# Attention rounds on TensorE: the older unit's value products ahead of the turning of probabilities

## The chip, the cores and the metric

The kernel runs on one core of a Trainium2 chip. The metric is the device time of one execution in microseconds (us), the slowest core's, which here is the only one. The profile comes from one further execution on the same kind of chip, recorded by the hardware profiler.

## What is computed

One forward pass at batch 1, 256 tokens and width 1024, in float32, through two blocks. The first has one layer: a mixer of forgetting attention (8 heads) and stick-breaking attention (8 heads), a cross-attention to 256 memory rows (4 heads of 256), and a mixture of 16 experts. The second has two layers, each a mixer of four groups and a gated feed-forward; a second stream of 256 context tokens runs beside the first in layer 0 only. Only the attentions matter here. Cut to what matters:

```python
def _forgetting_attention(q, k, v, f_logit):          # "fox", 8 heads of 64, blocks of 128 queries
    logits = einsum('bhqd,bhkd->bhqk', q_blk, kh) * scale + c_blk[..., None] - c[:, :, None, :]
    p = softmax(where(kpos <= qpos, logits, -inf)); return einsum('bhqk,bhkd->bhqd', p, vh)

def _memory_cross_attention(...):                     # "cross", 4 heads of 256, 256 memory rows
    p = softmax(einsum('bshd,bmhd->bhsm', q, k) * 256 ** -0.5)
    o = einsum('bhsm,bmhd->bshd', p, v)

# second block, each layer: groups A, C and D, 4 heads each
window_gqa(...)            # A: scores within a band and over the context, softmax with a sink, values
diff_weights(...)          # C: two softmaxes of 32-wide heads, w = p[0] - lam * p[1], values
neighbourhood_attn(...)    # D: 8x16 neighbourhood with a bias, and the context, softmax, values
```

## The kernel before

Each engine has a program of its own, written out in order, and they meet only at semaphores. An engine carries out its instructions in that order, so whatever stands behind a waiting instruction waits too. The names below ending in `_ready`, `_done` or `_turned` are such signals.

The four softmax attentions ("fox", "cross", "mix" of layer 0 and "mix" of layer 1) share one routine per engine: `pe_attention` on TensorE (PE), `act_attention` on ScalarE (ACT), `dve_attention` on VectorE (DVE). The work is cut into **units**: a block of 128 queries of one head or of two. fox has 8 units, cross 8, mix layer 0 has 32 (stream 0: C 8, A 4, D 4, with 512 keys; stream 1 the same with 256 keys), mix layer 1 has 16 (C 8, A 4, D 4, 512 keys). A unit has one or two score matrices (`subs`) and one or two probability matrices (`parts`): fox, A and D have two of each; C has two score matrices and one part; cross one of each. A **group** is the units whose outputs share PSUM bank 0 (in cross, banks 0 and 1 in turn).

The routines run in **steps**, step i being one pass of the loop over all units and three more. In step i

- PE writes the scores of unit i (L1051, extra terms L1055); does a small turn for the modulation vectors (L749, "ada"); turns the probabilities of unit i-2 with the identity matrix, 128x128 block by block, into bank 2 or 3 (L1067); multiplies the turned probabilities of unit i-3 with the values into the group's bank (L1084); then does what `fill` brings (ada products L742 in the first steps, and matmuls of the two norms, L1329, L1365, L1380);
- DVE takes the row maximum of unit i (L1126, for A with the sink L1129, L1130), then scales the probabilities of unit i-1 (L1144, or L1148 and L1150 for C), then, when a group of cross, A or D is complete, makes the low half of its output (L1157);
- ACT does the exponentials of unit i (L1097), copies the turned probabilities of unit i-2 from PSUM into `work` or `prob_turned` (L1109), and empties the bank of a complete group (L1171, L1175, L1179).

Who waits for whom, as far as the change touches it:

- a turning waits for its scaled probabilities (`probs_ready`, DVE) and for the ACT copy of the part two before it (`pT_ready`), because parts alternate between banks 2 and 3;
- value products wait for the copy of the last part of their unit (`pT_ready`), and in a new group for the bank being emptied: by ACT (`act_out`), after cross, A or D by DVE too (`dve_out`);
- the exponentials of unit i write into one of four buffers `prob(s)`. The score matrix four before must have been turned (`probs_turned`). With two score matrices a unit that is the turning of unit i-2, which PE does in the same step;
- scores wait for the exponentials four score matrices back (`exp_ready`; three back in cross).

In C, value products come only in every second step, for two units at once. After each attention the next stage waits for its last group; after the mixes these are the output projections ("wout2", L663 to L665).

Of the kernel before, what the change touches and what calls it, by code (L numbers as in the profile page):

```python
# [14 lines left out]
P = 128  # L15
# [204 lines left out]
def mixer_program(nc, a, out, counts):  # L220
# [6 lines left out]
    with ExitStack() as ctx:  # L227
# [3 lines left out]
        def signal(name):  # L231
            return Signal(ctx, nc, name, counts)
# [42 lines left out]
        bank = [ctx.enter_context(nc.psum_tensor(f"bank{i}", [P, 512], F32)) for i in range(4)]  # L275
# [3 lines left out]
        def const(name):  # L279
            off, n = CONST_AT[name]  # L280
            v = cst[:, off:off + n]
            return v.broadcast_to([P, P]) if n == 1 else v

        ident = const("ident")
# [64 lines left out]
        probs_ready = signal("probs_ready")  # L349
        probs_turned = signal("probs_turned")  # L350
        pT_ready = signal("pT_ready")
# [71 lines left out]
        def scores(qk, nk, extra=()):  # L423
            return dict(qk=qk, nk=nk, extra=extra)

        def part(sub, o, vals, lam=None):
            return dict(sub=sub, pv=[(o, vals)], lam=lam)
# [12 lines left out]
        def out_at(g, h, t):  # L440
            return bank[g["bank"]][head_rows(h), ((h % 4) // 2) * S + t * P:((h % 4) // 2) * S + t * P + P]

        fox_units, cross_units, mix_units = [], [], [[], []]
        for h in range(0, FOX_H, 2):
            if h % 4 == 0:
                g = group(("fox", h // 4))
            for t in range(ST):
                nk = (t + 1) * P
                subs, parts = [], []
# [7 lines left out]
        for h in range(X_HEADS):  # L457
            g = group(("cross", h), 2)
            for t in range(ST):
                s = scores([(xq[:, 2 * h + c, t * P:(t + 1) * P], xk[:, 2 * h + c, :]) for c in range(2)], S)  # L460
                pv = [(bank[g["bank"]][:, c * S + t * P:c * S + t * P + P],
                       [xv[:, b, (2 * h + c) * P:(2 * h + c + 1) * P] for b in range(ST)]) for c in range(2)]
                parts = [dict(sub=0, pv=pv, lam=None)]
                cross_units.append(dict(subs=[s], parts=parts, now=parts, group=("cross", h), last=t == 1))
        for l in range(LAYERS):
            for stream in range(2 if l == 0 else 1):
                lo = stream * S
                nk = 2 * S - lo
# [3 lines left out]
                for h in range(0, 4, 2):  # L472
                    for t in range(ST):
                        waiting = []
                        for x in (h, h + 1):
                            subs = []
# [3 lines left out]
                            parts = [part(0, out_at(g, x, t), [vc2[:, b, x * HD:(x + 1) * HD] for b in blocks], l)]  # L480
# [4 lines left out]
                for pair in ((0, 3), (1, 2)):  # L485
                    for t in range(ST):
                        subs, parts = [], []
                        for i, h in enumerate(pair):
                            kv = slice((h // 2) * HD, (h // 2) * HD + HD)
                            extra = []  # L490
                            if stream == 0:
# [5 lines left out]
                                                 last=pair == (1, 2) and t == 1,  # L497
                                                 sink=slice(l * 4 + pair[0], l * 4 + pair[1] + 1, step)))
                g = group(("D", l, stream))
                for h in range(0, 4, 2):  # L500
                    for t in range(ST):
                        subs, parts = [], []
                        for x in (h, h + 1):
                            extra = []
                            if stream == 0:
# [4 lines left out]
                                                 last=h == 2 and t == 1))  # L510
# [16 lines left out]
        prob = lambda s: work[:, (s % NP_) * 512:(s % NP_) * 512 + 512]  # L527
# [227 lines left out]
        def pe_ada_turn_left(pe):  # L755
            while ada_turn_left:
                pe_ada_turn(pe, ada_turn_left.pop())
# [282 lines left out]
        def pe_attention(pe, units, phase, fill):  # L1040

            ring, first = score_ring(phase), units[0]["s"][0]
            for i in range(len(units) + 3):
                if i < len(units):
                    unit = units[i]
                    for n in range(len(unit["subs"][0]["qk"])):
                        for s, sc in zip(unit["s"], unit["subs"]):
                            if n == 0 and s - first >= ring:
                                pe.wait_ge(*exp_ready.at(s - ring))
                            q, k = sc["qk"][n]  # L1050
                            last = pe.matmul(score_bank(phase, s)[:, 0:sc["nk"]], q, k, start=n == 0,  # L1051
                                             stop=n == len(sc["qk"]) - 1)
                    for s, sc in zip(unit["s"], unit["subs"]):
                        for left, right, c0, width in sc["extra"]:
                            last = pe.matmul(score_bank(phase, s)[:, c0:c0 + width], left, right, start=False, stop=True,  # L1055
                                             skip_group_check=True)
                    last.then_inc(*scores_ready.mark(unit["u"]))
                pe_ada_turn_left(pe)
                if 2 <= i < len(units) + 2:
                    unit = units[i - 2]  # L1060
                    nb = unit["subs"][0]["nk"] // P
                    for p in unit["parts"]:
                        pe.wait_ge(*probs_ready.at(p["p"]))
                        if p["p"] >= 2:
                            pe.wait_ge(*pT_ready.at(p["p"] - 2))
                        for b in range(nb):
                            last = pe.transpose(bank[2 + p["p"] % 2][:, b * P:(b + 1) * P],  # L1067
                                                prob(p["s"])[:, b * P:(b + 1) * P], ident)
                        last.then_inc(*probs_turned.mark(p["p"]))
                if i >= 3 and units[i - 3]["now"]:  # L1070
                    unit = units[i - 3]
                    g = groups[unit["group"]]
                    pe.wait_ge(*pT_ready.at(unit["now"][-1]["p"]))
                    if g["no"] >= g["banks"]:
                        emptied = by_no[g["no"] - g["banks"]]
                        pe.wait_ge(*act_out.at(("group", emptied)))
                        if emptied[0] in ("cross", "A", "D"):
                            pe.wait_ge(*dve_out.at(("group", emptied)))
                    for n in range(len(unit["now"][0]["pv"])):
                        nb = len(unit["now"][0]["pv"][n][1])  # L1080
                        for b in range(nb):
                            for p in unit["now"]:
                                o, vals = p["pv"][n]
                                last = pe.matmul(o, vals[b], by_block(p["p"])[:, b, :], start=b == 0, stop=b == nb - 1)  # L1084
                    last.then_inc(*pv_done.mark(unit["u"]))
                fill(i)

        def act_attention(act, units, phase, fill=lambda i: None):
# [955 lines left out]
        def _(pe):  # L2044
# [16 lines left out]
            pe.wait_ge(*dve_misc.at("forget"))  # L2061
            pe.wait_ge(*dve_misc.at("cond"))
            pe_attention(pe, fox_units, "fox", lambda i: pe_ada_step(pe, "fox", i))
            pe.wait_ge(*act_out.at(("group", ("fox", 1))))
            pe.wait_ge(*exp_ready.at(fox_units[-1]["s"][-1]))
# [13 lines left out]
            for j in range(4):  # L2079
                pe_tile(pe, ("xq", j), lambda c: pe_late(("xattn",))(pe, c) if j == 0 else None)  # L2080
                if j == 0:
                    pe_norm(pe, ("xattn",))
            pe.wait_ge(*dve_out.at(("xq", 3)))
            pe_attention(pe, cross_units, "cross", lambda i: pe_ada_step(pe, "cross", i))
            pe.wait_ge(*dve_out.at(("group", ("cross", 3))))
            for j in range(4):
# [25 lines left out]
            for l in range(LAYERS):  # L2112
# [21 lines left out]
                def fill(i, l=l):  # L2134
# [3 lines left out]
                    run_plan(l, "pe")(pe, i)  # L2138

                pe_attention(pe, mix_units[l], ("mix", l), fill)  # L2140
                for step in range(len(mix_units[l]) + 3, 60):
                    run_plan(l, "pe")(pe, step)
# [385 lines left out]
```

## Time and profile before

| | |
|---|---|
| median of 3 runs | 1779.58 us (1769.25 to 1780.74) |
| the profiled execution | 1777.42 us, of which its span is 1775.4 us |
| PE matmul busy | 1649.5 us, 93% of the span |
| DVE, ACT busy | 920.4 us, 688.5 us |
| share of the chain that ended last on PE | 84% |
| the four softmax attentions, us from the span's start | fox 105 to 147, cross 284 to 315, mix layer 0 800 to 915, mix layer 1 1464 to 1537 |

Times of rows are microseconds from the span's start. A row of the timeline is one merged set of instructions, with its start, its duration and, in brackets, how long the engine stood idle before it and what released it.

### The profile page before, as it was taken

To read this page: it belongs to the slowest core of one execution; us is meant where nothing else is said; L and a number is where in the kernel's file an instruction comes from. 1 tells how busy PE (TensorE), PEld (TensorE's weight loads), DVE (VectorE), ACT (ScalarE), POOL (GpSimd) and SP (SyncE) were. 2 spreads that over 40 slices of the span, in tenths; PEclk is the share of its full clock that TensorE was granted. 3 is DMA by queue.
4 is the path that set the end of the run, shared out by engine and by line. 5 is a ranking of instruction groups with operands and counts; after the bars stand their busy time and mean duration, and the time that the engine had idled before them with its cause. 6 is when DMAs were issued, how large, how long until landed. Compare 5 with 4: busy or idle time off the path is not lost.

```text
span 1775.4 us, 26046 instructions
## 1 busy us (share of the span) xinstructions
PE 1649.5 (93%) x11189; PEld 1427.8 (80%) x11189; DVE 920.4 (52%) x1249; ACT 688.5 (39%) x985; POOL 224.8 (13%) x203
## 2 busy tenths in 40 slices
PE   6999999999999998999688999999997998889997
PEld 5986898999999986875456878878876894789997
DVE  4621654665655553876745433323226767465554
ACT  4524543444433333225642322222223426543433
POOL 3001100020000013990200000000000690000000
PEclk8998999999999998999788999999998998989999
DMA  7466457355455533244204243343333330145552
GB/s 271 144 214 213 136 173 258 122 146 188 165 166 178 179 119 119 95 150 160 24 24 143 95 142 119 119 139 104 117 118 92 119 102 18 44 131 183 190 167 72
DMA packets 228892, 242.28 MB, mean 136 GB/s; under 512 B 13033, under 2 KB 222409, under 8 KB 228777
## 3 DMA queue, kind: packets, MB, share of 16 engines
q1 hardware_dynamic: 226672, 238.02, 40.8%
q0 software_dynamic: 1568, 2.37, 1.4%
q8 instruction: 89, 1.46, 0.3%
q10 hardware_dynamic: 536, 0.22, 0.1%
q14 instruction: 27, 0.21, 0.0%
HBM read 239.54 MB, written 1.05 MB: 136 GB/s over the span
## 4 chain that ended last, share of the span: by engine, by line
PE 84%; DVE 8%; ACT 4%; issue 2%; DMA 1%; ACTq 0%; POOL 0%; DVEq 0%
PE bank L663 21%; PE bank L665 20%; PE bank L664 20%; PE score_banks L1051 2%; PE bank L1084 2%; PE score_banks L1597 2%; DVE small L1126 2%; PE score_banks L1598 2%; PE score_banks L1599 2%; PE bank L1067 1%; PE bank L719 1%; PE score_banks L1055 1%; PE bank L720 1%; PE bank L721 1%; PE bank L742 1%
## 5 line engine op out<-in xcount | busy, mean ns | idle before, releaser
L652 DVE TENSOR_TENSOR w_lo<-raw,w_hi 128x2048 fp32r<-128x2048 f32 (+1 forms) x175 | 405.4, 2321 | 299.9 <-ACT w_hi L638 299.4
L663 PE MATMUL bank<-xn_hi,w_hi 128*128 128x256 f32 (+1 forms) x1248 | 416.5, 334 | 16.0 <-DVE w_lo L652 8.0
L664 PE MATMUL bank<-xn_lo,w_hi 128*128 128x256 f32 (+1 forms) x1248 | 412.4, 330 | 0.0
L665 PE MATMUL bank<-xn_hi,w_lo 128*128 128x256 f32 (+1 forms) x1248 | 412.2, 330 | 0.0
L638 ACT ACTIVATE w_hi<-raw 128x2048 fp32r<-128x2048 f32 (+1 forms) x176 | 332.0, 1888 | 160.0 <-PE bank L665 99.1
L663 PE MATMUL bank<-hid_hi,w_hi 128*128 128x256 f32 (+1 forms) x928 | 284.6, 307 | 3.5 <-DVE w_lo L652 1.3
L664 PE MATMUL bank<-hid_lo,w_hi 128*128 128x256 f32 (+1 forms) x928 | 282.4, 304 | 0.0
L665 PE MATMUL bank<-hid_hi,w_lo 128*128 128x256 f32 (+1 forms) x928 | 282.3, 304 | 0.0
L663 PEld LDWEIGHTS bank<-xn_hi,w_hi 128*128 128x128 f32 x1248 | 239.4, 192 | 41.8 <-issue 16.2
L665 PEld LDWEIGHTS bank<-xn_hi,w_lo 128*128 128x128 f32 x1248 | 239.3, 192 | 21.3
L664 PEld LDWEIGHTS bank<-xn_lo,w_hi 128*128 128x128 f32 x1248 | 239.5, 192 | 20.5
L663 PEld LDWEIGHTS bank<-hid_hi,w_hi 128*128 128x128 f32 x928 | 178.3, 192 | 13.4 <-DVE hid_lo L1556 1.8
L665 PEld LDWEIGHTS bank<-hid_hi,w_lo 128*128 128x128 f32 x928 | 178.2, 192 | 7.0
L664 PEld LDWEIGHTS bank<-hid_lo,w_hi 128*128 128x128 f32 x928 | 178.3, 192 | 6.8
L1550 ACT ACTIVATE hid_hi<-work 128x512 fp32r<-128x512 f32 (+1 forms) x38 | 28.8, 757 | 216.6 <-DVE work L1568 145.6
L1486 DVE SCALAR_TENSOR_TENSOR xT<-bank,mod,xT 128x256 f32<-128x256 f32 x96 | 40.6, 478 | 134.9 <-PE bank L665 134.9
L1126 DVE TENSOR_REDUCE small<-score_banks 128x2 f32<-128x1024 f32 (+3 forms) x64 | 57.9, 906 | 97.8 <-PE score_banks L1055 54.0
L1097 ACT ACTIVATE work<-score_banks,small 128x512 f32<-128x512 f32 (+2 forms) x120 | 68.6, 578 | 98.1 <-DVE small L1126 72.5
L2035 POOL MEMSET sq<- 128x1144 f32 x2 | 2.1, 1054 | 797.4 <-DVE xn_lo L985 797.4
L1469 ACT ACTIVATE proj<-bank 128x512 f32<-128x512 f32 (+1 forms) x60 | 31.4, 558 | 183.2 <-PE bank L665 177.1
L1309 POOL TENSOR_SCALAR proj<-sq,vec 128x512 f32<-128x512 f32 (+1 forms) x60 | 94.1, 1569 | 5.9
L719 PE MATMUL bank<-xn_hi,w_hi 128*128 128x256 f32 (+1 forms) x160 | 56.8, 355 | 22.6 <-DVE xn_lo L985 12.6
(294 smaller groups left out, 2430.8 us busy)
## 6 DMA issues: line engine op xcount, KB each, us to landing
raw<-in_w_ada SPq DMA_DIRECT2D x48, 1024.0 KB, 5.1
raw<-in_w_in SPq DMA_DIRECT2D x30, 1024.0 KB, 5.1
raw<-in_w_gate SPq DMA_DIRECT2D x22, 1024.0 KB, 5.1
raw<-in_w_up SPq DMA_DIRECT2D x22, 1024.0 KB, 5.1
raw<-in_w_exp_gate SPq DMA_DIRECT2D x16, 1024.0 KB, 5.4
raw<-in_w_exp_up SPq DMA_DIRECT2D x16, 1024.0 KB, 5.4
raw<-in_w_exp_down SPq DMA_DIRECT2D x16, 1024.0 KB, 4.8
raw<-in_w_down SPq DMA_DIRECT2D x16, 1024.0 KB, 4.7
```

Source lines behind the costliest of these rows:

```text
L638: act.activation(w_hi[:, i % HIGH_SLOTS, 0:k * cols], raw[:, r % RAW_SLOTS, 0:k * cols], ACT.Copy)\
L652: dve.tensor_tensor(w_lo[:, r % RAW_SLOTS, 0:k * cols], raw[:, r % RAW_SLOTS, 0:k * cols], w_hi[:, i % HIGH_SLOTS, 0:k * cols].bitcast(F32 ...
L663: pe.matmul(o, s_hi, m_hi, start=i == 0, stop=False)
L664: pe.matmul(o, s_hi, m_lo, start=False, stop=False)
L665: last = pe.matmul(o, s_lo, m_hi, start=False, stop=i == n - 1)
L719: pe.matmul(o, hi[:, c, cs], xn_hi[:, c, ts], start=first, stop=False, skip_group_check=True)
L1051: last = pe.matmul(score_bank(phase, s)[:, 0:sc["nk"]], q, k, start=n == 0, stop=n == len(sc["qk"]) - 1)
L1084: last = pe.matmul(o, vals[b], by_block(p["p"])[:, b, :], start=b == 0, stop=b == nb - 1)
L1097: last = act.activation(prob(s)[:, 0:nk], score_bank(phase, s)[:, 0:nk], ACT.Exp, bias=nmax(s), accum_out=rsum(s))
L1126: ins = dve.tensor_reduce(nmax(s0, n), src, AX.X, ALU.max, negate=True)
L1309: own.ready(pool.tensor_scalar(term, src(1, k), w, None, ALU.mult))
L1486: last = dve.scalar_tensor_tensor(out=x, in0=src, scalar=mod[:, name[1], g, s:s + 1], in1=x, op0=ALU.mult, op1=ALU.add)
```

## The change

In `pe_attention` the block of value products of unit i-3 is moved up, ahead of the block that turns the probabilities of unit i-2. No instruction is added or taken away, and the other engines' programs are the same.

```diff
                 pe_ada_turn_left(pe)
-                if 2 <= i < len(units) + 2:
-                    unit = units[i - 2]
...
-                        for b in range(nb):
-                            last = pe.transpose(bank[2 + p["p"] % 2][:, b * P:(b + 1) * P],
-                                                prob(p["s"])[:, b * P:(b + 1) * P], ident)
-                        last.then_inc(*probs_turned.mark(p["p"]))
                 if i >= 3 and units[i - 3]["now"]:
                     unit = units[i - 3]
...
                     last.then_inc(*pv_done.mark(unit["u"]))
+                if 2 <= i < len(units) + 2:
+                    unit = units[i - 2]
+                    nb = unit["subs"][0]["nk"] // P
+                    for p in unit["parts"]:
+                        pe.wait_ge(*probs_ready.at(p["p"]))
+                        if p["p"] >= 2:
+                            pe.wait_ge(*pT_ready.at(p["p"] - 2))
+                        for b in range(nb):
+                            last = pe.transpose(bank[2 + p["p"] % 2][:, b * P:(b + 1) * P],
+                                                prob(p["s"])[:, b * P:(b + 1) * P], ident)
+                        last.then_inc(*probs_turned.mark(p["p"]))
                 fill(i)
```

In the changed kernel the turnings are L1083 and the value products L1073. Where group C gives way to group A in mix layer 0, stream 0 (steps 10 and 11), PE's rows move like this:

```order
 L1051 MATMUL score_banks<-proj 128x512 x2
 L1055 MATMUL score_banks<-cst 128x128 x2
 L749 MATMUL bank<-cst,ada_sums 128x2 x2
-L1067 MATMUL bank<-cst,work 128x128 x8
-L1084 MATMUL bank<-prob_turned,proj 64x128 x8
+L1073 MATMUL bank<-prob_turned,proj 64x128 x8
+L1083 MATMUL bank<-cst,work 128x128 x8
 L1051 MATMUL score_banks<-proj 128x512 x2
 L1055 MATMUL score_banks<-cst 128x128 x2
-L1067 MATMUL bank<-cst,work 128x128 x8
-L1084 MATMUL bank<-work 64x128 x8
+L1073 MATMUL bank<-work 64x128 x8
```

The eight value products of the older unit now stand between the scores and the turnings, so the turnings come one block later. The same piece with its waits, at the change from group A to group D in stream 1 (step 31):

```order
-L1067 MATMUL bank<-cst,work 128x128 [waits pT_ready,probs_ready]
-L1067 MATMUL bank<-cst,work 128x128
-L1067 MATMUL bank<-cst,work 128x128 [waits pT_ready,probs_ready]
-L1067 MATMUL bank<-cst,work 128x128
-L1084 MATMUL bank<-work,proj 64x128 [waits dve_out,act_out,pT_ready]
-L1084 MATMUL bank<-work,proj 64x128 x3
+L1073 MATMUL bank<-work,proj 64x128 [waits dve_out,act_out,pT_ready]
+L1073 MATMUL bank<-work,proj 64x128 x3
+L1083 MATMUL bank<-cst,work 128x128 [waits pT_ready,probs_ready]
+L1083 MATMUL bank<-cst,work 128x128
+L1083 MATMUL bank<-cst,work 128x128 [waits pT_ready,probs_ready]
+L1083 MATMUL bank<-cst,work 128x128
```

The wait of the value products for the emptied bank (`act_out`, `dve_out`) stood behind the turnings and now stands ahead of them. The end of mix layer 1 (of before its last two steps, of the change its last four):

```order
-L1067 MATMUL bank<-cst,work 128x128 x8
-L1084 MATMUL bank<-work,proj 64x128 x8
-L1084 MATMUL bank<-prob_turned,proj 64x128 x8
+L1073 MATMUL bank<-work,proj 64x128 x8
+L1083 MATMUL bank<-cst,work 128x128 x8
+L1073 MATMUL bank<-prob_turned,proj 64x128 x8
+L1083 MATMUL bank<-cst,work 128x128 x8
+L1073 MATMUL bank<-work,proj 64x128 x8
+L1083 MATMUL bank<-cst,work 128x128 x8
+L1073 MATMUL bank<-prob_turned,proj 64x128 x8
```

The last unit's turnings stood two blocks of value products before the end; now only one block, which needs those very turnings, comes behind them.

## Rows read from the trace of the kernel before

**Rows 1.** The page: the span, and busy time by engine.

```profile
span 1775.4 us, 26046 instructions
PE 1649.5 (93%) x11189; PEld 1427.8 (80%) x11189; DVE 920.4 (52%) x1249; ACT 688.5 (39%) x985; POOL 224.8 (13%) x203
```

**Rows 2.** Windows: stretch, length, PE, PEld, DVE, ACT, POOL busy, clock, DMA, GB/s.

```profile
105.00:147.00 42.00, 39.66 (x380) 28.66 (x380) 10.28 (x41) 15.07 (x60) 0.00 (x0) 1.00 0.73 236
...
795.00:915.00 120.00, 95.99 (x721) 58.23 (x722) 84.16 (x181) 75.83 (x202) 16.07 (x21) 0.86 0.32 78
...
1480.00:1540.00 60.00, 48.60 (x357) 32.89 (x358) 39.65 (x78) 37.46 (x84) 0.00 (x0) 0.89 0.00 1
```

**Rows 3.** Waits of PE, 795 to 915: total, times, longest.

```profile
PE bank L1067 <- DVE work L1150: 7.0, 4, 5.5
PE bank L1067 <- ACT prob_turned L1109: 4.8, 4, 2.0
PE bank L1067 <- ACT work L1109: 4.3, 3, 2.7
```

**Rows 4.** Timeline of PE, fox, last two steps: turning, then both value products.

```profile
145.11 0.64 PE L1067 MATMUL bank<-cst,work 128*128 128x128 f32 x4
145.68 0.44 PE L1084 MATMUL bank<-work,proj 128*64 128x128 f32 x4
146.28 0.66 PE L1084 MATMUL bank<-prob_turned,proj 128*64 128x128 f32 x8 [0.16 <-ACT prob_turned L1109]
```

**Rows 5.** Timeline of PE, cross, step 9 value products.

```profile
311.58 1.06 PE L1084 MATMUL bank<-prob_turned,proj 128*128 128x128 f32 x8
```

**Rows 6.** Timeline, mix layer 0, step 11: C gives way to A.

```profile
826.80 1.12 PE L1067 MATMUL bank<-cst,work 128*128 128x128 f32 x8
...
827.02 0.61 ACT L1175 ACTIVATE sq<-bank 128x512 f32<-128x512 f32 x1
...
827.85 1.09 PE L1084 MATMUL bank<-work 128*64 128x128 f32 x16
```

**Rows 7.** Timeline, mix layer 0, steps 14 and 15: A gives way to D.

```profile
837.43 0.69 ACT L1097 ACTIVATE work<-score_banks,small 128x512 f32<-128x512 f32 x1 [1.41 <-DVE small L1126]
...
838.77 1.08 ACT L1109 ACTIVATE prob_turned<-bank 128x512 f32<-128x512 f32 x2
...
839.99 1.04 PE L1067 MATMUL bank<-cst,work 128*128 128x128 f32 x8
...
846.64 1.09 PE L1084 MATMUL bank<-work,proj 128*64 128x128 f32 x16 [0.58 <-DVE xn_lo L1157]
```

**Rows 8.** Timeline, mix layer 0, step 17: exponential behind its turning.

```profile
855.98 1.98 PE L1084 MATMUL bank<-work,proj 128*64 128x128 f32 x16
...
856.09 0.47 ACT L1097 ACTIVATE work<-score_banks,small 128x256 f32<-128x256 f32 x1 [0.23 <-PE bank L1067]
```

**Rows 9.** Timeline, mix layer 0, step 24: turning, exponential, value products.

```profile
877.82 0.69 PE L1067 MATMUL bank<-cst,work 128*128 128x128 f32 x2 [5.46 <-DVE work L1150]
...
881.16 1.12 PE L1084 MATMUL bank<-work,proj 128*64 128x128 f32 x8 [2.65 <-ACT work L1109]
...
881.94 0.48 ACT L1097 ACTIVATE work<-score_banks,small 128x256 f32<-128x256 f32 x1
```

**Rows 10.** Timeline, mix layer 0, steps 33 and 34.

```profile
910.52 1.12 PE L1067 MATMUL bank<-cst,work 128*128 128x128 f32 x4
...
911.25 0.81 ACT L1109 ACTIVATE prob_turned<-bank 128x256 f32<-128x256 f32 x2 [1.29 <-PE bank L1067]
...
911.57 1.12 PE L1084 MATMUL bank<-work,proj 128*64 128x128 f32 x8
```

**Rows 11.** Timeline of PE, mix layer 1, steps 8, 15 and 17.

```profile
1493.68 1.98 PE L1084 MATMUL bank<-work,proj 128*64 128x128 f32 x16 [1.50 <-ACT work L1109]
...
1524.88 1.09 PE L1084 MATMUL bank<-work,proj 128*64 128x128 f32 x16 [0.58 <-DVE xn_lo L1157]
...
1534.26 1.17 PE L1084 MATMUL bank<-work,proj 128*64 128x128 f32 x16
```

More of the change, by code:

```diff
@@ L1058, in pe_attention @@
                 pe_ada_turn_left(pe)
-                if 2 <= i < len(units) + 2:
-                    unit = units[i - 2]
[L1061 to L1065, printed above, removed]
-                        for b in range(nb):
-                            last = pe.transpose(bank[2 + p["p"] % 2][:, b * P:(b + 1) * P],
-                                                prob(p["s"])[:, b * P:(b + 1) * P], ident)
-                        last.then_inc(*probs_turned.mark(p["p"]))
                 if i >= 3 and units[i - 3]["now"]:
```

## Prediction

> **What bounds the kernel now.** First the page: TensorE (PE) is busy for 1649.5 of 1775.4 us [rows 1], so the kernel as a whole is PE's, and only a stretch in which PE waits can be changed by an order. The windows show where the attentions stand [rows 2]: in fox PE is busy for 39.66 of 42 us at a granted clock of 1.00, in mix layer 0 for 95.99 of 120 us at 0.86, in mix layer 1 for 48.60 of 60 us at 0.89. The same PE instructions stand before and after the change, so it can only lengthen or shorten those 24 and 11 us of waiting. Then the waits of PE in mix layer 0 [rows 3]: its turnings (L1067) wait for the scaling on DVE (7.0 us, of which 5.5 in one place) and for ACT's copies (4.8 and 4.3 us); the value products (L1084) wait once for 2.65 us [rows 9]. The turning is thus where the rounds meet the other engines, and it is what is moved back. The next stage needs the last group of each attention, so time lost in these rounds is not made up later; I find no cover behind them.
>
> **The change, part by part.** Nothing is removed or added. In each step the value products of unit i-3 go first and the turning of unit i-2 comes later by their length. Three prices hang on that.
>
> *Steps in which nothing waits: nothing.* In fox, in cross and in C of stream 0 PE runs from one block to the next, the copies were made a step earlier, and the sum of the blocks is the same. The cover is PE's own work: about 4 us in a step. Exponentials that wait for the later turning end well within the step.
>
> *The end of an attention.* Before, the value products of the last but one unit ran under ACT's copy of the last turning. In fox the turning starts at 145.11, the first products at 145.68, the last products at 146.28 after 0.16 us of waiting [rows 4]. With the products first, turning, copy and last products all move back by their length, taken as the distance 0.37 to 0.44: fox **+0.4**. In cross the same block takes 1.06 us [rows 5]; it lies between 0 and 1.1 there, since ACT is also busy with weights, and I take the middle, **+0.5**. In mix layer 0 a block takes 1.12 us at the lower clock, and the copy began at 911.25, under the products that started at 911.57 [rows 10]: between 0.6 (full clock) and 1.3 (two copies uncovered): **+1.1**. In mix layer 1 the block takes 1.17 us [rows 11]: **+1.0**.
>
> *A change of group.* The first value products of a new group wait until the bank is emptied. Before, the turnings (1.04 to 1.12 us) filled that wait; now they stand behind it. From C to A the turning ran from 826.80, ACT emptied the bank from 827.02 to 827.63, the products started at 827.85 [rows 6]. The products stay where they are, the turning follows at 828.9: +1.05. From A to D the products waited 0.58 us for DVE's low half and started at 846.64 [rows 7]; again they stay, and the turning comes behind: +1.05. In stream 1 turnings are half as long, or as long at half the clock: two changes at +0.8. Layer 1 has both of the long kind, the second with the same 0.58 us [rows 11]: +1.05 each. Together **+5.8**. Bounds: nothing, if copies that were late for the turnings too hide it, and 1.12 six times, 6.7.
>
> *A longer loop.* The exponential of unit i needs the buffer that the turning of unit i-2 frees, ACT then copies that turning, and PE needs the copy. Before, the copies came at 838.77 to 839.85, just in time for a turning at 839.99, of which the first half needs only the first copy [rows 7]; now the value products stand there and need both. Per long step two exponentials (837.43 to 838.77, 1.34 us), two copies (1.08) and values (1.02 from start to start) make about 4.2 us with the first half of the turning (0.5) and hand-overs, against some 4.0 of PE work: **+0.4** over the few steps. Where the key blocks shrink from 512 to 256 the loop is bare: in step 17 PE ran values from 855.98 for 1.98 us, and ACT's exponential at 856.09 had waited for the turning before them [rows 8]. With the turning 1.9 us later, exponential and copies are too, and only part of it has cover in PE's scores and in the drained backlog: between 0 and 1.9, I take **+0.8**.
>
> *The layer norm.* It lies on DVE and ACT and holds up PE. In layer 0, step 24, the turning had waited 5.46 us for DVE and ran at 877.82, the value products waited until 881.16 for ACT's copy, the exponential ran at 881.94 [rows 9]. Now the products come first, still at 881.16, and the turning only at 882.3; the exponential, and all of ACT behind it, waits until 882.95: **+1.0**. In layer 1, step 8, the products started at 1493.68 after a wait for ACT and took 1.98 us [rows 11]; the turning that stood before them now comes at 1495.6 and takes 0.7 to 1.1: **+1.0**, bounds 0 and 2.6.
>
> Sum: 0.4 + 0.5 + 1.1 + 1.0 for the ends, 5.8 for the groups, 0.4 + 0.8 for the loop, 1.0 + 1.0 for the norms = 12.0 us. Some of these meet: a loss at a change of group starts the next wait later too. I take 0.7 off, **+11.3**. Against the profiled execution of 1777.42 us (span 1775.4 [rows 1] and 2 around it) that is 1788.7; that execution lies 2.2 under the median of 1779.58, and against the median it is **1790.9 us**.
>
> At one place a page of the Trainium skill gives another price. The eight turnings at 839.99 take 1.04 us, 122 ns from one start to the next over 0.97 us [rows 7]. The Trainium skill, "TensorE: Matmul & The Clock Gate", section "Back-to-back issue gap", gives about 81 ns per matmul of 128 columns in a stream of weight loads and matmuls, as an estimate 0.65 us for the eight. By it the six changes of group would cost about 3.7 us in place of 5.8, and the forecast would be about 1788.8. The row decides, since it is this very block in float32.
>
> **The rivals.**
>
> *The clock falls more often* (chance 0.17). The granted clock is already 0.86 and 0.89 on average in the mixes [rows 2], that is partly at the lower of its levels of 2.4 and 1.2 GHz, and one block of value products took 1.98 us in place of 1.09 [rows 8, 11]. New waits of 1 to 2.5 us stand in stretches that ran at 1.00. If steps 15 to 17 of layer 0 and the D steps of layer 1 fell to 1.2 GHz, some 6 and 3 us of blocks would take twice as long: +9 on top, 1800. [...] Beside it stands the rule of the Trainium skill ("TensorE: Matmul & The Clock Gate", section "Loop structure matters more than you think"), which speaks against this change: waits between matmuls let the array go cold, dense work keeps it warm. [...]
>
> *Slack after all* (0.19). If the late turnings find cover in ACT's and DVE's own delays, only the ends (3.0) and bits of the groups stay: +1 to +6, about 1783. For it speaks that PE's turnings already wait 9.1 us for ACT's copies in mix layer 0 [rows 3], and both blocks wait for the same copies there. Against it: these waits are what the value products would inherit, with the turnings behind them.
>
> *Faster* (0.07). Value products that are ready could fill the wait of a turning for DVE, 7.0 us in layer 0 [rows 3]. It decides where the copy is there before the scaled probabilities. The largest wait is no such place: its products waited 3.3 us longer than the turning, until 881.16 [rows 9]. The remaining 1.5 us lie in three waits, and one of them has no value products in its step (C has them in every second). It can give at most the 1.5 us: 1778 if all else cost nothing.
>
> **How the numbers follow.** The sum as forecast has the rest, 0.57; its own range is +7 to +16, 1787 to 1796. The range reaches to the slack (about 1781) and into the clock's case (1803), which leaves out the faster case, the cheapest slack and the dearest clock, about 0.2 in all. A change of under 1% (17.8 us) is about what a measurement of this kernel can tell from none. The sum, the slack and most of the faster case lie within it, and a part of the clock's: 0.82 within 1%, 0.16 slower, 0.02 faster.
>
> **What the profile afterwards would show.** (1) Fox and cross: the same start-to-start times in their steps, and ends later by 0.4 and 0.5. (2) Value products (then L1073) wait where turnings did: L1073 behind ACT L1109, ACT L1175 and DVE L1157, and hardly a wait of L1083 for ACT. (3) At each change of group the products start at the old distance from the bank's emptying, the turnings follow. (4) Exponentials (L1097) wait for PE L1083 more often than before. (5) Mix layer 0 longer by about 7, mix layer 1 by about 4. (6) All other stages as long as before. Wrong would be: a stage outside the four attentions that changes, value products that fill waits for DVE, or a granted clock that falls in stretches that had 1.00.

## The result, and the profile after

The changed kernel takes 1794.04 us (median of 4 runs, 1790.61 to 1799.26), the kernel before 1779.26 us (median of 4, 1769.25 to 1780.74). The ratio is 1.0098, with a 95% interval of 1.0052 to 1.0143: 17.4 us slower, where +11.3 and 1790.9 us were forecast. The profiled execution took 1795.65 us with a span of 1793.6. Two executions of the experiments below, one of the kernel before and one of a changed kernel, took three times as long (5.5 and 5.3 ms) and are left out of every number.

The page of the changed kernel, the lines that answer to [rows 1]:

```profile
span 1793.6 us, 26046 instructions
PE 1657.2 (92%) x11189; PEld 1429.6 (80%) x11189; DVE 921.1 (51%) x1249; ACT 688.9 (38%) x985; POOL 224.7 (13%) x203
```

The span grew by 18.2 us with the same instructions. PE's busy time grew by 7.7 us without more work: blocks at the lower clock take longer. The windows (columns as in [rows 2]) of fox and mix layer 0:

```profile
105.00:148.00 43.00, 39.81 (x376) 28.96 (x378) 10.27 (x41) 15.00 (x59) 0.00 (x0) 1.00 0.72 230
795.00:928.00 133.00, 104.53 (x740) 61.22 (x732) 86.32 (x182) 77.22 (x206) 18.36 (x22) 0.80 0.30 75
```

Mix layer 0 has 28.5 us without matmul, 24.0 before [rows 2], and its granted clock fell from 0.86 to 0.80. From the first scores to the last value products of each attention (in fox to the first matmul behind them, L1189), and between them, the two timelines give:

| us | fox | to cross | cross | to mix 0 | mix 0 | to mix 1 | mix 1 | rest |
|---|---|---|---|---|---|---|---|---|
| before | 42.19 | 136.53 | 29.00 | 469.85 | 129.47 | 551.59 | 71.19 | 240.14 |
| after | 43.47 | 136.72 | 29.74 | 469.89 | 140.53 | 554.02 | 74.24 | 239.28 |
| difference | +1.3 | +0.2 | +0.7 | 0.0 | **+11.1** | **+2.4** | +3.0 | -0.9 |

The +11.1 rests on one execution of each kernel, and the one before had a fall of the clock of its own: from 852 to 858 us, in steps 16 and 17, it stood at 0.50, and the value products of [rows 8] took 1.98 us there. A kernel below that has the old order in this layer (the one with the change in mix layer 1 alone) ran the same steps at 1.00 and the layer in 126.3 us. Its value products of step 16, at the full clock:

```profile
848.66 1.09 PE L1074 MATMUL bank<-prob_turned,proj 128*64 128x128 f32 x16
```

In step 16 the kernel before took 1.62 us for them. So this layer's time in a single profile is good to about 3 us and no better.

The waits of PE in mix layer 0, 795 to 930 us (total, times, longest), beside [rows 3]:

```profile
PE bank L1073 <- ACT work L1109: 9.9, 4, 7.1
PE bank L1073 <- ACT prob_turned L1109: 6.9, 7, 1.7
PE bank L1073 <- DVE xn_lo L1157: 5.8, 2, 3.7
PE bank L1073 <- ACT sq L1175: 2.1, 2, 1.1
...
PE bank L1083 <- DVE work L1150: 0.5, 1, 0.5
```

The waits have moved from the turnings to the value products (L1073), as forecast. The same for ACT; its exponentials had waited for PE's turnings for only 2.9 us in three places before:

```profile
ACT work L1097 <- PE bank L1083: 32.8, 19, 4.0
```

This is the line that matters most. What the wait does is seen where A gives way to D in mix layer 0. PE's timeline there, and below it ACT's:

```profile
851.01 1.98 PE L1073 MATMUL bank<-work,proj 128*64 128x128 f32 x16 [2.08 <-DVE xn_lo L1157]
852.92 1.80 PE L1083 MATMUL bank<-cst,work 128*128 128x128 f32 x8
...
856.61 1.09 PE L1073 MATMUL bank<-prob_turned,proj 128*64 128x128 f32 x16 [1.26 <-ACT prob_turned L1109]
...
860.43 1.09 PE L1073 MATMUL bank<-work,proj 128*64 128x128 f32 x16 [1.08 <-ACT work L1109]
...
864.26 1.09 PE L1073 MATMUL bank<-prob_turned,proj 128*64 128x128 f32 x16 [1.08 <-ACT prob_turned L1109]
```

```profile
854.13 0.69 ACT L1097 ACTIVATE work<-score_banks,small 128x512 f32<-128x512 f32 x1 [3.99 <-PE bank L1083]
...
855.47 1.08 ACT L1109 ACTIVATE prob_turned<-bank 128x512 f32<-128x512 f32 x2
```

The value products wait for the bank to be emptied, the turning waits behind them, ACT's exponential waits 3.99 us for that turning, ACT's copies stand behind the exponential, and the next value products wait for the copies. In the kernel before the turning ran at once, and the exponential at the same place waited for DVE alone:

```profile
848.26 0.69 ACT L1097 ACTIVATE work<-score_banks,small 128x512 f32<-128x512 f32 x1 [2.49 <-DVE small L1126]
```

### The profile page after: what moved, and what is told of

It reads as the page before. It is cut to its first block, busy times and chain, and to the rows that moved or that the text cites. A ratio compares the mean times of both kernels' runs of the same rounds, so it can differ in the third digit from the quotient of the medians.

```text
span 1793.6 us, 26046 instructions
## 1 busy us (share of the span) xinstructions
PE 1657.2 (92%) x11189; PEld 1429.6 (80%) x11189; DVE 921.1 (51%) x1249; ACT 688.9 (38%) x985; POOL 224.7 (13%) x203
## 4 chain that ended last, share of the span: by engine, by line
PE 83%; DVE 7%; ACT 6%; issue 2%; DMA 1%; ACTq 0%; POOL 0%; DVEq 0%
PE bank L663 20%; PE bank L664 20%; PE bank L665 20%; PE bank L1073 2%; PE score_banks L1051 2%; PE score_banks L1597 2%; PE score_banks L1598 2%; PE score_banks L1599 2%; PE bank L1083 1%; PE bank L719 1%; PE bank L720 1%; PE bank L721 1%; DVE w_lo L652 1%; ACT work L1097 1%; ACT w_hi L638 1%
```

## The experiments

The ratio is always to the kernel before on the same chip, with its 95% interval. A second figure is needed here. Single executions of the kernel before spread over 18 us, and they do so with the mean granted clock: over 67 of them the mean is 1776 us at a clock of 0.9575, and 0.01 less of clock goes with 12 us more. So for each kernel the mean clock of its executions is given too, and what is left of its mean time over 1776 us when 12.2 us per 0.01 are taken off. The two columns add up to the difference of the means, which can lie 1 to 2 us from what the ratio gives. This division is by correlation, not by an edit: a wait that brings the clock down is the cause of both. For the filled kernels it says little, since their clock is held up by matmuls that nobody needs.

| kernel | ratio | interval | clock | by clock, us | left, us | runs |
|---|---|---|---|---|---|---|
| the change | 1.0098 | 1.0052–1.0143 | 0.954 | +5 | +14 | 4 |
| only in mix layer 0 | 1.0070 | 1.0045–1.0095 | 0.954 | +5 | +8 | 6 |
| only in mix layer 1 | 1.0015 | 0.9998–1.0032 | 0.959 | -1 | +5 | 12 |
| without the edges | 1.0043 | 1.0021–1.0066 | 0.957 | 0 | +7 | 12 |
| only the edges | 1.0072 | 1.0044–1.0100 | 0.953 | +6 | +6 | 6 |
| change, six buffers | 1.0047 | 1.0029–1.0065 | 0.957 | +1 | +7 | 11 |
| change, six buffers, other place | 1.0049 | 1.0028–1.0070 | 0.957 | +1 | +7 | 8 |
| before, six buffers | 1.0000 | 0.9985–1.0015 | 0.957 | 0 | 0 | 12 |
| change, bank waited for once | 1.0095 | 1.0075–1.0116 | 0.954 | +4 | +12 | 6 |
| change, old order in steps 11–23 | 1.0073 | 1.0047–1.0098 | 0.954 | +4 | +9 | 6 |
| change, waits filled | 1.0117 | 1.0095–1.0140 | 0.961 | -5 | +25 | 4 |
| change, waits filled less | 1.0068 | 1.0043–1.0093 | 0.961 | -5 | +17 | 9 |
| before, waits filled less | 0.9973 | 0.9953–0.9994 | 0.965 | -9 | +5 | 12 |

A single profile is read with the same care. In several of these profiles the clock was at 0.54 to 0.58 from 780 to 795 us, where before and after had 1.00, and the first four steps of mix layer 0 took 4.6 us longer. So phases are compared from the scores of step 4 to the last value products: 116.1 us before, 127.1 after (+11.0). Further profiles of the old order in this stretch show 116.1 (six buffers) and 112.9 us (change in mix layer 1 alone), and of the new order 126.4 (bank waited for once) and 123.4 us (change in layer 0 alone). The loss of the layer is thus between 7 and 14 us, and a difference of under 3 us between two profiles of it shows nothing.

**Where the loss sits.** Both blocks became small functions, and a condition chooses their order:

```diff
-                if i >= 3 and units[i - 3]["now"]:
+                def values():
...
+                def turning():
...
+                for block in ((values, turning) if phase == ("mix", 0) else (turning, values)):
+                    block()
```

> The value products go ahead of the turnings in mix layer 0 alone; fox, cross and mix layer 1 keep the old order. By the changed kernel's trace mix layer 0 runs from 2.9 us late at its step 8 to 13.6 us late at its last value products, so 10 to 11 us should come from here if what the trace shows is the mechanism. By the prediction's own sum it would be 6.8 us. If the delay were one execution's accident of the clock, under 4 us.

Measured: +12.4 us, mix layer 0 from step 4 at 123.4 us (+7.3), the way to mix layer 1 +2.3. With `phase == ("mix", 1)`:

> The new order in mix layer 1 alone. The changed kernel's trace has 3.1 us from the first scores (16.0 us late) to the last value products (19.1 us late); the prediction's sum had about 4. If the places were additive, mix layers 0 and 1 together give 13 to 14 us and fox and cross the last 2. The rival that the loss comes from one stage after another getting out of step would give 0 here.

Measured: +2.7 us, mix layer 1 at 73.9 us (+2.7). The two parts and the +2.0 that the timelines show in fox and cross make 17.1 of the 17.4 us. The parts add up, as far as intervals of 3 to 4 us on each can tell, and layer 0 has most of it.

**Edges or steady steps.** "Edges" are the first value products of each group and the steps after the last scores. The condition is

```diff
+                for block in ((values, turning) if (i < len(units) and not (
+                        i >= 4 and units[i - 3]["group"] != units[i - 4]["group"])) else (turning, values)):
```

and its opposite for the other kernel.

> The new order in all four attentions, but the old one in the first value step of each new group and in the last three steps of each attention. Theory of the prediction: changes of group (5.8 us) and ends (3.0 us) carry most of the loss, so it should fall from 15 to about 4 to 6 us. Rival: the longer loop of turning, exponentials, copies and value products carries it, with the lower clock after it; then 9 to 12 us remain.

> The complement: the old order everywhere except in the first value step of each new group and the last three steps of each attention, which have the new one. Theory of the prediction: 7 to 9 us slower than before. Rival (the loop carries the loss): 3 to 5 us, since the old order around an edge takes the delay back.

Measured: +7.6 us without the edges and +12.8 us with only the edges. Neither expectation was met: the first lies between its two theories, the second above both. Together they are 20.4 us for a whole of 17.4, which is within their intervals. In the profiles mix layer 0 from step 4 is longer by 5.6 and 3.7 us, mix layer 1 by 0.1 and 2.4. In layer 1 the loss is thus all at the edges: without them it takes 71.2 us, as before, where three profiles of the old order lie between 71.1 and 71.3. In layer 0 both parts cost, also the steady steps, for which the prediction had only +1.2 and the norm's +1.0; which of the two costs more is not shown, since the profiles differ by less than 3 us. Of the +12.8 of the edges 6 us go with the clock, by the correlation.

**The loop through the buffers.** The exponential of unit i writes where the turning of unit i-2 has read. Six buffers in place of four move this to the turning of unit i-3:

```diff
-        NP_, NT = 4, 4
-        prob = lambda s: work[:, (s % NP_) * 512:(s % NP_) * 512 + 512]
+        NP_, NT = 6, 4
+        prob = lambda s: (work[:, (s % NP_) * 512:(s % NP_) * 512 + 512] if s % NP_ < 4 else
+                          work[:, 3584:4096] if s % NP_ == 4 else sixth[:, :])
```

In these two kernels the fifth buffer lies over the row of ones that the router reads, so the routing is computed from other numbers; the work is the same.

> The changed kernel with six buffers for the probabilities in place of four: an exponential of unit i then waits for the turning of unit i-3, a step earlier, in place of the turning of unit i-2 in its own step. If the loop through the late turning (ACT waited 31.9 us in 18 places in mix layer 0 for turnings, 2.9 us before) carries the loss, 5 to 9 of the 15 us go away. If the changes of group carry it, at most 2 us go away, since there the turning itself and not the exponential is late.

> The kernel of before with the same six buffers. In its order only 2.9 us of exponentials' waits for turnings stand in mix layer 0, so both theories expect 0 to 2 us of gain. A gain of the size that the changed kernel gets would say that the buffers help whatever the order.

Measured: 1.0047 for the change and 1.0000 for before. The extra buffers give the old order nothing and take half of the loss from the new one: some 9 of the 17 us. Mix layer 0 from step 4 is 119.0 us, 8 us less than after; mix layer 1 stays at 74.5. The same with buffers that overlay nothing in use:

> The changed kernel with six buffers for the probabilities once more, the fifth now where no other stage keeps a row: its instructions and their shapes are those of the run with six buffers before. If that run's time was the order's and not an effect of what it computed, this one is again 7 to 9 us slower than before (half of the loss gone) and mix layer 0 takes 131 to 134 us.

Measured: 1.0049, mix layer 0 from step 4 at 117.3 us. The exponentials (here L1100) no longer wait for turnings but for DVE, as before the change. ACT's waits in mix layer 0 of this kernel:

```profile
ACT work L1100 <- DVE small L1129: 18.6, 15, 2.5
ACT work L1100 <- DVE small L1133: 11.0, 5, 2.7
```

In mix layer 0 both kernels with six buffers lie 8 us and more under the change, and 4 and 6 us under the shorter profile of the new order (123.4 us). The times say the same without a profile: 1.0029 to 1.0065 and 1.0028 to 1.0070 with six buffers, 1.0075 to 1.0116 for the change with the bank waited for once (below), which else is the change itself. So the loop is the main cause in mix layer 0. Part of what stays is at the edges, where the value products (here L1076) still wait for the bank with the turnings behind them; two of PE's waits there:

```profile
PE bank L1076 <- DVE xn_lo L1160: 6.2, 2, 4.0
...
PE bank L1076 <- ACT sq L1178: 2.4, 2, 1.6
```

**The steps where the loop was expected to bite.** The old order in steps 11 to 23 of mix layer 0 (D of stream 0, C of stream 1, the shrinking key blocks), by the same condition:

> The changed kernel with the old order in steps 11 to 23 of mix layer 0 (the end of A, D of stream 0 and C of stream 1), the new one everywhere else. In the changed kernel's trace the first scores of step 24 come 7.2 us later than before, counted from the start of the phase, and the rest of the phase adds 3.8. If the longer loop in these steps is the main loss, these 7 us go and about 8 of the 15 remain. If the granted clock alone made the phase long, less than 3 us go.

Measured: 1.0073 against 1.0098, 4 us less where 7 were expected, and mix layer 0 from step 4 at 119.9 us, 7.2 less than after but only 3.5 less than in the other profile of the new order. That these 13 steps hold most of the layer's loss is thus likely and not shown: the intervals of the two ratios overlap.

**A price per block.** In steps in which nothing waits the changed kernel is still slower by a little. One candidate was the wait for the bank, which the code repeats in every value product block:

```diff
-                    if g["no"] >= g["banks"]:
+                    if g["no"] >= g["banks"] and (i == 3 or i - 3 == min(
+                            n for n, x in enumerate(units) if x["group"] == unit["group"] and x["now"])):
```

> The changed kernel, in which the value products wait for the emptied bank only in the first value step of a group; later steps of the group do not repeat the wait, which is long fulfilled there. In the trace a D step without any idle time takes 4.17 us, against 4.02 before, with the same instructions. If the three waits ahead of the products cost the time (scores to products 1.06 us, scores to turnings 0.97 before), steps shrink by about 0.1 and the whole by 1 to 3 us. If the boundary itself between values and turnings costs, nothing changes.

Measured: 1.0095, no change, and a block of value products still starts 1.06 us after the scores before it. The repeated waits cost nothing that these runs could show, and what the boundary's price comes from stays open.

**The clock.** To see what the falls of the clock cost, PE was given spare matmuls in front of its long waits, each of 512 columns into a bank that nobody reads just then:

```diff
+                n = {(("mix", 0), 16): 2, (("mix", 0), 17): 2, (("mix", 0), 18): 2, (("mix", 0), 20): 2,
+                     (("mix", 0), 24): 13, (("mix", 1), 8): 10}.get((phase, i), 0)
...
+                for _ in range(n):
+                    pe.matmul(spare[:, :], ident, cst[:, 0:512], start=True, stop=True)
```

> The changed kernel with extra matmuls of 512 columns that write to free banks while TensorE would wait: two each ahead of the value products in steps 16, 17, 18 and 20 of mix layer 0, thirteen in step 24, ten in step 8 of mix layer 1. They compute nothing that is used. If the granted clock falls because TensorE stands idle there, and the half clock from 871 to 908 us costs time, it stays at 1.00 longer and the kernel gets 3 to 6 us faster than the changed one. If these stretches are bound by DVE and ACT whatever the clock, 0, or 1 us slower from the extra work.

Measured: 1.0117, no gain (+20.8 us). Each spare matmul took 0.88 us and not the 0.47 that I had reckoned with, so the 13 of step 24 overran the wait by 2.7 us. They did hold the clock: 1.00 from 855 to 890, where the change had 0.55 from 870 to 885. Shorter fillings, in the change (1, 1, 1, 1, 8 and 5, and 1 in step 32) and in the kernel before (6 and 2 in step 24, 1 in step 32, 3 and 1 in step 8 of layer 1; there a turning's two waits also change places, to let the spare matmuls stand between them):

> The changed kernel with fewer extra matmuls in its waits (one each in steps 16, 17, 18, 20 and 32 of mix layer 0, eight in step 24, five in step 8 of mix layer 1). One such matmul took 0.88 us, twice what was reckoned, so the fuller version ran 2.7 us past the wait. If the lower clock costs time in these stretches, this one is 3 to 5 us faster than the changed kernel; if DVE and ACT bind there whatever TensorE's clock, it is within 1 us of it.

> The kernel of before with extra matmuls in its long waits (eight in step 24 of mix layer 0, one in step 32, four in step 8 of mix layer 1), to hold the granted clock at its upper level through 877 to 897 us. If TensorE's clock costs time there, 2 to 4 us faster than before, which would beat both kernels; if not, the same within 1 us.

Measured: 1.0068 for the change, whose interval overlaps that of the unfilled one; and 0.9973 (0.9953 to 0.9994) for the kernel before, 4.8 us faster and the fastest of all kernels here. Windows of PE in the kernel before, unfilled, over the layer norm waits of both mixes (busy time, clock, DMA share, GB/s):

```profile
855.00:900.00 45.00, 33.42 (x189) 0.73 0.09 10
1490.00:1520.00 30.00, 26.37 (x192) 0.89 0.00 1
```

and with the waits filled:

```profile
855.00:900.00 45.00, 37.91 (x212) 0.89 0.10 12
1490.00:1520.00 30.00, 26.80 (x206) 1.00 0.01 1
```

Not all of the first difference is the filling's. The layer's first spare matmul stands at 869.8 us, and the clock ahead of it, in steps 16 and 17, differs from one profile of the old order to the next. Over the 30 us from the scores of step 24 the clock is 0.66 in three kernels of the old order without fillings and 0.83 with them; it still fell to 0.50, from 884 to 894.

Its timeline at step 24 shows six spare matmuls (each recorded as two), the turning, two more of them, and the value products:

```profile
869.80 5.42 PE L1046 MATMUL bank<-cst 128*128 128x512 f32 x12
875.26 0.44 PE L1074 MATMUL bank<-cst,work 128*128 128x128 f32 x2
875.53 1.88 PE L1046 MATMUL bank<-cst 128*128 128x512 f32 x4
878.60 0.66 PE L1092 MATMUL bank<-work,proj 128*64 128x128 f32 x8 [1.18 <-ACT work L1117]
```

The eight value products took 0.66 us in place of 1.12 [rows 9]: they ran at 2.4 and not at 1.2 GHz. Mix layer 0 fell from 129.5 to 125.4 us, but 3.1 of these 4.1 us lie ahead of step 24, before any spare matmul of the layer: from the scores of step 24 to the last value products it is 39.9 us, and 40.8 in the three kernels without fillings. Mix layer 1 fell from 71.2 to 67.7 us, of which 0.7 lies in its first four steps, ahead of the fillings, too. So the profiles give the fillings about 1 us in layer 0 and 3 us in layer 1.

## Why the prediction was right or wrong

The direction and the range held. The sum was 6 us smaller than the measured 17.4, and some of its parts were wrong. Of the total alone one could not say so, since its interval goes from +9 to +25 us and has the +11.3 in it; the change with the bank waited for once, +13 to +21, has not.

**Waits pass to the value products: right.** L1073 waits behind ACT L1109, ACT L1175 and DVE L1157, and L1083 hardly waits at all, as point 2 said. Exponentials wait for PE L1083 as point 4 said, but 19 times and 32.8 us.

**The ends: right in mechanism.** In fox the last step now runs without anything under the copy:

```profile
146.27 0.44 PE L1073 MATMUL bank<-work,proj 128*64 128x128 f32 x4
146.64 0.66 PE L1083 MATMUL bank<-cst,work 128*128 128x128 f32 x4
147.82 0.66 PE L1073 MATMUL bank<-prob_turned,proj 128*64 128x128 f32 x8 [0.53 <-ACT prob_turned L1109]
```

From the block before the turning to the last products it is 1.55 us, where it was 1.17 from the turning to the last products [rows 4]: +0.38 for +0.4. Mix layer 0 from step 31 to its end is 13.19 us for 11.46: +1.7, for the 1.1 of the end and the 0.8 of the change of group that lies in it.

**"Steps in which nothing waits: nothing": wrong, if small.** Fox lost 0.89 us ahead of its end: 0.09 in each of its steps with both blocks, and 0.27 in a longer wait of L749 for ACT. Cross lost 0.045 in each. In the D steps the changed kernel's blocks stand like this:

```profile
839.38 1.13 PE L1055 MATMUL score_banks<-aux,cst 128*128 128x256 f32 x4
...
840.44 1.09 PE L1073 MATMUL bank<-work 128*64 128x128 f32 x16
841.46 1.10 PE L1083 MATMUL bank<-cst,work 128*128 128x128 f32 x8
842.49 1.13 PE L1051 MATMUL score_banks<-proj 64*128 64x512 f32 x4
```

and in the kernel before, with the rest in [rows 7]:

```profile
839.02 1.13 PE L1055 MATMUL score_banks<-aux,cst 128*128 128x256 f32 x4
...
840.96 1.09 PE L1084 MATMUL bank<-prob_turned,work 128*64 128x128 f32 x16
841.98 1.13 PE L1051 MATMUL score_banks<-proj 64*128 64x512 f32 x4
```

From scores to the next block it is now 1.06 us (0.97 before), from the turnings to what follows 1.03 (0.97 before). The same blocks in another sequence cost 0.15 us more a step, and the step takes 4.17 us for 4.02. The step of the prediction that failed here is "the sum of the blocks is the same". Why a block takes longer behind another neighbour no run shows. I had forecast 4.2 us for this step, but from a loop of waits; the number was right and its reason was not, for these products wait for nothing.

**"A longer loop, +1.2": mis-sized, and the main miss.** The mechanism was named, with its place in steps 14 to 18. Its size was not right: six buffers, which cut just this loop, give back some 9 us of the whole, where the term had 1.2. The row on which the +0.8 was worked out, 1.98 us in step 17 [rows 8], was itself of the lower clock, which two of the four profiles of the old order show in this step and two do not. Three things were left out. The loop runs at 3.82 us a step with about 1.1 us of idle PE in each of steps 16 to 18 (the three rows after the change from A to D above), where I counted only the first turning. The kernels with the change in layer 0 alone and with the bank waited for once have the same 3.82 us. Each late bank or late norm feeds it: the turning that stands behind a waiting block of value products holds up ACT, which holds up the next copies. I costed the changes of group and the norm as if only their own block were late. That this is how the 9 us come together is read from the timeline and not shown by an edit. And a fifth change of group in layer 0, from D of stream 0 to C of stream 1, has no term in the sum: its first value products, in step 20, waited 1.24 us for ACT's copy after the change and not at all before.

**"The changes of group, +5.8", the ends, and "the norms, +1.0 each": somewhat too large by the profiles, not by the time.** With only the edges in the new order mix layer 0 is 3.7 us longer from step 4, where the sum had 3.7 for changes of group and 1.1 for the end; layer 1 is 2.4 longer, for 2.1 and 1.0. By the time of its runs this kernel lost 12.8 us (7.8 to 17.8) where the sum had 8.8 for all ends and changes of group. The norm of layer 1 costs nothing alone: without the edges this layer is as long as before. In layer 0 the norm's wait moved as the sum had it, but it cannot be told from a lower clock:

```profile
873.27 3.62 PE L1380 MATMUL bank<-proj,cst 128*128 128x512 f32 x4
...
889.75 1.12 PE L1073 MATMUL bank<-work,proj 128*64 128x128 f32 x8 [7.09 <-ACT work L1109]
```

The block L1380 ahead of the wait took 3.62 us, and 1.88 at the full clock in the second kernel with six buffers (3.43 in the first). From the scores of step 21 to those of step 24 this execution took 2.3 us longer than that of the kernel with the change in layer 0 alone (10.2 for 7.9), whose clock from 871 to 881 us was 0.83 where here it was 0.52. So some 2 of the 11 us belong to this execution's clock there, and not to each; against that, the kernel before lost 3 us to its own fall in steps 16 and 17.

The 122 ns of a turning in [rows 7] against the figure of 81 ns in the Trainium skill, "TensorE: Matmul & The Clock Gate", section "Back-to-back issue gap": eight turnings stand 1.02 us from start to start in the changed kernel, so the row was the better price, and the skill's would have made the forecast worse.

**"All other stages as long as before": wrong in one place.** The way from mix layer 0 to layer 1 is 2.4 us longer, since the projection behind the layer starts at the lower clock. Matmuls of the changed kernel from its start:

```profile
928.60 0.79 PE L663 MATMUL bank<-xn_hi,w_hi 128*128 128x512 f32 x1 [1.42 <-DVE xn_lo L1157]
...
930.05 0.63 PE L663 MATMUL bank<-xn_hi,w_hi 128*128 128x512 f32 x1
...
932.61 0.54 PE L663 MATMUL bank<-xn_hi,w_hi 128*128 128x512 f32 x1
...
933.47 0.40 PE L663 MATMUL bank<-xn_hi,w_hi 128*128 128x512 f32 x1
```

Triples that stand 1.3 to 1.5 us apart at first take 0.7 to 0.8 from 933.5 on, as they did from the start in the kernel before. That the new waits at the layer's end brought the clock down is the likely reading: the kernels with only layer 0 and with only the edges lose 2.3 and 3.0 us here too, and the one without the edges 0.4. The prediction had named two signs of being wrong that appear here, a stage outside the attentions that changes and a clock that falls where it had been 1.00.

**The rivals.** "The clock falls more often" was right in part. I had it as a case of its own at 0.17; it is a share of every case: of the change's 17 to 18 us about 5 go with the lower mean clock, by the correlation. Its own price, +9, was too large, and the places were others: around the norm's wait and at the layer's end. Of the steps that I had named only step 15 was hit (0.66 from 850 to 855 us, then 1.00 up to 870), and not in each execution: the kernel with the change in layer 0 alone ran it at the full clock. The rule set beside it (the Trainium skill, same page, section "Loop structure matters more than you think") is borne out: dense work in the waits brought the clock of the 30 us from step 24 on from 0.66 to 0.83, and made the kernel before faster. "Slack" and "faster" are out: no value products filled a wait for DVE, and the late turnings found no cover.

What stays open: how much of the edges' +12.8 us is a wait and how much clock. Its six executions, at 0.953, are few, and the profiled one was the shortest. Open too are the price at a block's boundary, and how the layer's loss divides among its steps.

## What to carry to other kernels

Before an engine's block is moved back, follow who waits for what it frees, and whether that engine's queue also holds the input of the block that now stands ahead: such a ring can hand on each late event from step to step, so its price can be several times the length of the block (here some 9 us, where 1.2 had been reckoned). Two more buffers in the ring are a cheap test of it. And where a long wait of TensorE leads into dense float32 work, the waiting costs twice, once itself and once in the slower blocks behind it. Spare matmuls that end before the wait does can then pay: 0.3% in the kernel before; in the changed one no gain was shown.

## What was unexpected of the hardware

- The order of blocks has a price with no wait in the trace: 0.06 to 0.09 us at the boundary of a block with another neighbour in mix layer 0, 0.15 us in a long step there, 0.09 in one of fox and 0.045 in one of cross.
- The time of an execution follows its mean granted clock, some 12 us per 0.01 over 67 executions of one unchanged kernel, and that is nearly all of its spread of 18 us (correlation -0.97).
- A float32 matmul of 512 columns takes 0.88 to 0.91 us at the full clock, recorded as two of about 0.45.
